# Writing the lower parts of the weights over the loaded pieces in a one-core decoder step

## The reference, cut to what matters

```python
# two groups of tokens: a prompt (512) and 8 samples of 8 tokens; 2 layers; all in float32
for layer in range(2):
    x = layer_norm(ALPHA * x + 0.5 * swiglu(x, *f1), ...)     # D_MODEL 1024, D_FF 2816
    mix = attention_and_retention(x) if layer == 0 else s5_layer(x)
    x = layer_norm(ALPHA * x + mix, ...)
    x = layer_norm(ALPHA * x + 0.5 * swiglu(x, *f2), ...)

def swiglu(x, w_gate, w_up, w_down):
    return (jax.nn.silu(x @ w_gate) * (x @ w_up)) @ w_down
```

## Time and profile before

| | |
|---|---|
| median of 3 runs | 2473.53 us (2472.99 to 2474.01) |
| profiled execution, its own time | 2471.69 us |
| its span, first to last instruction | 2470.0 us |
| granted TensorE clock, mean | 0.986 |
| PE busy | 2366.2 us (96%) |
| DVE busy | 1622.1 us (66%) |
| ACT busy | 1081.8 us (44%) |
| POOL busy | 465.0 us (19%) |
| moved by DMA | 417.85 MB, 169 GB/s on average |

### The profile page before, as it was taken

One profiled execution on the slowest core, in us unless ns is written; L12 is line 12 of the kernel. 1 busy time (PEld: TensorE's weight loads), 2 busy tenths in 40 slices (PEclk: granted clock), 3 DMA queues, 4 the chain that ended last, 5 costly groups with the idle time before them and its releaser, 6 DMA issues.

```text
span 2470.0 us, 46567 instructions
## 1 busy us (share of the span) xinstructions
PE 2366.2 (96%) x18943; PEld 2252.9 (91%) x18943; DVE 1622.1 (66%) x2539; ACT 1081.8 (44%) x1633; POOL 465.0 (19%) x535
## 2 busy tenths in 40 slices
PE   7989999999899999999999999999999999999998
PEld 6988998999789777888999999999999998999997
DVE  4796776666675656678677476477556594487555
ACT  3433344433554433452454534554333537354332
POOL 4896720000300022200202001031002010221001
PEclk9999999999999999999999999999999999999998
DMA  8667776445345798544565555555554566554553
GB/s 176 174 173 205 196 194 193 136 116 146 111 148 177 239 308 259 147 131 121 170 180 163 171 161 184 177 166 145 155 153 138 189 184 212 156 164 145 152 147 106
DMA packets 676422, 417.85 MB, mean 169 GB/s; under 512 B 31570, under 2 KB 639698, under 8 KB 676210
## 3 DMA queue, kind: packets, MB, share of 16 engines
q1 hardware_dynamic: 669682, 394.51, 55.3%
q0 software_dynamic: 6528, 20.37, 2.7%
HBM read 396.04 MB, written 18.78 MB: 168 GB/s over the span
## 4 chain that ended last, share of the span: by engine, by line
PE 76%; DVE 13%; ACT 4%; issue 3%; DMA 2%; SPq 1%; POOL 1%; DVEq 0%; ACTq 0%; POOLq 0%
PE ps L270 21%; PE ps L272 20%; PE ps L271 20%; DVE w_lo L265 4%; PE ps L1004 2%; PE ps L1006 2%; PE ps L1005 2%; ACT w_hi L256 2%; PE ps L2410 1%; DMA w_raw<-in_ffn_w_up 1%; DVE h_lo L467 1%; DVE x L557 1%; PE ps L1742 1%; PE ps L1165 1%; PE ps L2393 1%
## 5 line engine op out<-in xcount | busy, mean ns | idle before, releaser
L265 DVE TENSOR_TENSOR w_lo<-w_raw,w_hi 128x1024 fp32r<-128x1024 f32 (+1 forms) x648 | 826.8, 1280 | 612.1 <-ACT w_hi L256 608.9
L270 PE MATMUL ps<-x_hi,w_hi 128*128 128x256 f32 (+1 forms) x3200 | 970.4, 303 | 32.3 <-DVE w_lo L265 18.9
L271 PE MATMUL ps<-x_lo,w_hi 128*128 128x256 f32 (+1 forms) x3200 | 955.3, 299 | 0.0
L272 PE MATMUL ps<-x_hi,w_lo 128*128 128x256 f32 (+1 forms) x3200 | 955.1, 298 | 0.0
L256 ACT ACTIVATE w_hi<-w_raw 128x1024 fp32r<-128x1024 f32 (+1 forms) x648 | 670.3, 1035 | 582.2 <-PE ps L272 419.1
L270 PEld LDWEIGHTS ps<-x_hi,w_hi 128*128 128x128 f32 x3200 | 615.8, 192 | 50.8 <-DVE w_lo L265 35.0
L271 PEld LDWEIGHTS ps<-x_lo,w_hi 128*128 128x128 f32 x3200 | 616.0, 192 | 1.1 <-issue 0.2
L272 PEld LDWEIGHTS ps<-x_hi,w_lo 128*128 128x128 f32 x3200 | 615.6, 192 | 0.0
L270 PE MATMUL ps<-h_hi,w_hi 128*128 128x256 f32 (+1 forms) x1408 | 423.2, 301 | 14.4 <-DVE w_lo L265 10.9
L271 PE MATMUL ps<-h_lo,w_hi 128*128 128x256 f32 (+1 forms) x1408 | 414.6, 294 | 0.0
L272 PE MATMUL ps<-h_hi,w_lo 128*128 128x256 f32 (+1 forms) x1408 | 414.6, 294 | 0.0
(11 more groups left out here) (281 smaller groups left out, 2137.7 us busy)
## 6 DMA issues: line engine op xcount, KB each, us to landing
w_raw<-in_ffn_w_gate SPq DMA_DIRECT2D x176, 512.0 KB, 4.3
w_raw<-in_ffn_w_up SPq DMA_DIRECT2D x176, 512.0 KB, 3.9
w_raw<-in_ffn_w_down SPq DMA_DIRECT2D x128, 512.0 KB, 3.9
w_raw<-in_w_in_ab SPq DMA_DIRECT2D x56, 512.0 KB, 3.8
w_raw<-in_ffn_w_down SPq DMA_DIRECT2D x64, 384.0 KB, 3.3
arena<-in_cache_k SPq DMA_DIRECT2D x64, 256.0 KB, 5.1
arena<-in_cache_v POOLq DMA_DIRECT2D x64, 256.0 KB, 5.0
w_raw<-in_w_out_ab SPq DMA_DIRECT2D x16, 512.0 KB, 3.8
```

What stands on the lines that cost most here:

```text
L265: dve.tensor_tensor(T.w_lo[:, u % RING, 0:n], T.w_raw[:, u % RAW, 0:n], T.w_hi[:, u % RING, 0:n].bitcast(F32), ALU.subtract).then_inc(T.w_ ...
L270: pe.matmul(out, w_hi, m_hi, start=first, stop=False)
L271: pe.matmul(out, w_hi, m_lo, start=False, stop=False)
L272: return pe.matmul(out, w_lo, m_hi, start=False, stop=last)
```

## The change

The ring `w_raw` gets six places and lies on the same bytes as `w_lo`: the subtraction writes its result over the loaded piece. `w_hi` stays at three places, so the memory taken is the same (36 KB a partition). Of three semaphores for loads in flight nothing changes. The load of w(u) no longer waits for the subtraction of w(u-3) but for two other things: that PE is through with w(u-6), and that ACT has rounded w(u-3). `AHEAD` goes from 5 to 6.

```diff
-RAW, RING = 3, 3
+LOADING, RINGS, RING = 3, 6, 3
 LEAD = 2
...
-    T.w_raw = sb("w_raw", [P, RAW, PIECE])
     T.w_hi = sb("w_hi", [P, RING, PIECE], F32R)
-    T.w_lo = sb("w_lo", [P, RING, PIECE], F32R)
+    here = (T.nc.sbuf_base + 31) // 32 * 32
+    T.w_lo = sb("w_lo", [P, RINGS, PIECE], F32R)
+    T.w_raw = T.nc.alloc_sbuf_tensor_at("w_raw", [P, RINGS, PIECE], F32, offset=here)
...
-        dst = T.w_raw[:, u % RAW, 0:a * b].rearrange("p (a b) -> p a b", a=a)
-        if u >= RAW:
-            sp.wait_ge(T.w_split.h, u - RAW + 1)
-        sp.dma_start(dst, src).then_inc(T.w_loaded[u % RAW].h, 16)
+        dst = T.w_raw[:, u % RINGS, 0:a * b].rearrange("p (a b) -> p a b", a=a)
+        if u >= RINGS:
+            sp.wait_ge(T.w_used.h, u - RINGS + 1)
+        if u >= LOADING:
+            sp.wait_ge(T.w_rounded.h, u - LOADING + 1)
+        sp.dma_start(dst, src).then_inc(T.w_loaded[u % LOADING].h, 16)
...
-AHEAD = RAW + LEAD
+AHEAD = RINGS
...
-            load_pieces(T, sp, RAW + 8)
+            load_pieces(T, sp, LOADING + 8)
             load_tables(T, M, sp, I)
```

More of the change, by code:

```diff
@@ L187, in open_trunk @@
     T.pieces, T.banks, T.emptied, T.releases = [], [], [], {}
-    T.w_loaded = [count(f"w_loaded{i}") for i in range(RAW)]
+    T.w_loaded = [count(f"w_loaded{i}") for i in range(LOADING)]
     T.w_rounded, T.w_split, T.w_used = map(count, ("w_rounded", "w_split", "w_used"))
@@ L252, in round_piece @@
     n = T.pieces[u].shape[1] * T.pieces[u].shape[2]
-    act.wait_ge(T.w_loaded[u % RAW].h, (u // RAW + 1) * 16)
+    act.wait_ge(T.w_loaded[u % LOADING].h, (u // LOADING + 1) * 16)
     if u >= RING:
         act.wait_ge(T.w_used.h, u - RING + 1)
-    act.activation(T.w_hi[:, u % RING, 0:n], T.w_raw[:, u % RAW, 0:n], ACT.Copy).then_inc(T.w_rounded.h, 1)
+    act.activation(T.w_hi[:, u % RING, 0:n], T.w_raw[:, u % RINGS, 0:n], ACT.Copy).then_inc(T.w_rounded.h, 1)
 def rest_piece(T, dve, u):
@@ L264, in rest_piece @@
     dve.wait_ge(T.w_rounded.h, u + 1)
-    dve.tensor_tensor(T.w_lo[:, u % RING, 0:n], T.w_raw[:, u % RAW, 0:n], T.w_hi[:, u % RING, 0:n].bitcast(F32),
+    dve.tensor_tensor(T.w_lo[:, u % RINGS, 0:n], T.w_raw[:, u % RINGS, 0:n], T.w_hi[:, u % RING, 0:n].bitcast(F32),
                       ALU.subtract).then_inc(T.w_split.h, 1)
@@ L298, in columns_times @@
         cols = slice(k * P, (k + 1) * P)
-        mm = product3(pe, out, T.w_hi[:, u % RING, cols], T.w_lo[:, u % RING, cols], m_hi(k), m_lo(k),
+        mm = product3(pe, out, T.w_hi[:, u % RING, cols], T.w_lo[:, u % RINGS, cols], m_hi(k), m_lo(k),
                       first and k == 0, last and k == kt - 1)
@@ L1001, in project_tensor @@
                 x_hi, x_lo = T.x_hi[:, kk, tile_cols(t)], T.x_lo[:, kk, tile_cols(t)]
-                w_hi, w_lo = T.w_hi[:, u % RING, cols], T.w_lo[:, u % RING, cols]
+                w_hi, w_lo = T.w_hi[:, u % RING, cols], T.w_lo[:, u % RINGS, cols]
                 out = T.ps[:, bank, 0:MIX]
@@ L2945, in _ @@
                 sp.dma_start(rows[:, t], x_prompt[t * P:(t + 1) * P, :]).then_inc(T.x_loaded[t].h, 16)
-            load_pieces(T, sp, RAW)
+            load_pieces(T, sp, LOADING)
             S5C.load(sp)
```

## The result

| | before | after |
|---|---|---|
| median | 2473.46 us (2472.99 to 2474.01, 4 runs) | 2503.9 us (2498.84 to 2507.36, 4 runs) |
| ratio, 95% interval | | 1.0126 [1.0111, 1.0142] |
| profiled execution, its own time | 2471.69 us | 2507.36 us |
| its span | 2470.0 us | 2505.7 us |
| granted TensorE clock, mean | 0.986 | 0.982 |

The change makes the kernel 30.4 us (1.3%) slower. The forecast was 7 us slower, with 17 at most. The profiled execution is the slowest of its four, 3.5 us over their median, so the two traces lie 35.7 us apart, 5.3 more than the medians.

The account below looks back on a forecast made before the run. PE was taken as the bound, with hardly any idle time. Key pages +11, S5 +4 and gains -8 made +7 us on 2471.69; with 1.84 us to the median, 2480.5 us, 0.3% slower. Range -4 (2470) to +17 us (2490).

Parts of the forecast that it names:

- The cost of writing over the operand: A cost of the subtraction writing over its loaded piece, unseen and left out of the range: about one in ten.
- The tables' 2.4 us: Near 60 us: w10 and the tables go 1.3 us earlier, w11 passes two small transfers; PE's 2.4 us wait can go.
- the first term: The tables' gain of 2.4 us, which the DVE-bound stretch from 113 to 162 us may swallow.
- w53 and w54: Near 207 and 214 us: w53 goes behind eight stores instead of eight and four; PE's waits of 3.0 and 2.4 us go.
- w67: Near 258 us: its load passes twelve stores; PE's wait of 2.9 us shrinks to about 0.4, gain 2.5 us.
- all else comes from `AHEAD`: Beyond the earlier gate, each side transfer stands behind one load more: loads gain by passing it, the side work loses.
- The 1.28 us per gate: A load's gate moves from the end of a subtraction to the end of its rounding, 1.28 us earlier on average.
- The pairs with exponentials: Key pairs 10, 18 and 26, issued late behind a rounding that follows five exponentials: 1.7, 5.1 and 4.3 us lost.
- The plain pairs: Other key pairs: pair 25 issued 2.6 us late, losing 1.6 us; about half have more in hand and cost nothing.
- full price: Rival with landings as before: losses 16 + 4.7, gains 4, so +17 us, 2490; included in the forecast's 0.60.
- Taps and decays: Second S5 stretch, octets 11 to 15: decays issued later behind a load; 1.0 us at octet 11, 3.9 us in all.
- made_rows: S5 transfers near 1937 us, with 0.4 and 1.8 us in hand: 0.8 us lost.

Follow-up runs that it names:

- e1_ahead5: The changed kernel with AHEAD 5 instead of 6, shared bytes and new gates kept: 2465.01 us, ratio 0.9973 to the kernel before.
- e2_order_alone: The kernel before with AHEAD one higher (6) and nothing else: 2523.48 us, ratio 1.0208.
- e4_bytes_alone: The changed kernel with the shared bytes kept, but the old gate (subtraction of w(u-3)) and AHEAD 5: 2473.12 us, ratio 0.9999 to the kernel before.
- h2_long_holds: The kernel before with PE held nine times between 1738 and 1865 us while GpSimd writes 56 columns: 2501.0 us, ratio 1.0106.
- e3_then5: The changed kernel with AHEAD 6 early and 5 from the key pages to the end: 2463.98 us, ratio 0.9965 to the kernel before.
- h1_short_holds: The kernel before with PE held nine times between 1738 and 1865 us while GpSimd writes 14 columns: 2480.48 us, ratio 1.0021.
- e6_s5b5: The changed kernel with AHEAD 6 up to the second S5 stretch and 5 from there on: 2493.52 us, ratio 1.0083 to the kernel before.

## Why the prediction was off, point by point

**Right: the gates, the place and the sign.** The new wait for PE never decides. SP waits for ACT's rounding, where it waited for DVE:

```profile
SPq L243 <- ACT w_hi L259: 1932.4, 605, 16.1
```

605 waits in place of 607, and the same total but for 2%. `e1_ahead5` and `e2_order_alone` show that the loss sits in `AHEAD` and nowhere else, as the step said. The cost of writing over the operand, for which I had left one chance in ten, is nothing (`e4_bytes_alone`).

**Gains: 8 us forecast, 8.2 in the trace, but not by the terms: that they met is luck.** The tables' 2.4 us were won and lost again. At 114 us PE waits for DVE, which is in S5 preparation and comes late to a subtraction:

```profile
107.40 3.73 DVE L2158 COPY arena<-s_powers 128x64 f32<-128x64 f32 x8
111.29 0.91 DVE L2161 MEMSET arena<- 16x1024 f32 x1 [0.15 <-issue]
112.36 0.91 DVE L2161 MEMSET arena<- 16x1024 f32 x1 [0.16 <-issue]
113.31 3.44 DVE L268 TENSOR_TENSOR w_lo<-w_raw,w_hi 128x1024 fp32r<-128x1024 f32 x2
```

The prediction had said that the DVE-bound stretch may swallow the first term, and kept it in the 8 all the same. (`h2_long_holds`, which there is still the kernel before, has a wait of 2.8 us at this place too, so it isn't the change's alone.) The others came out larger in the shift of PE: 6.7 us instead of 5.4 for w53 and w54, 2.5 for w67. But of the 9.1 us from w48 to w72 only 4.8 are idle time, where the terms had 7.9; 4.4 are the clock, whose granted share from 200 to 265 us is 1.00 after and 0.92 before. No term had that. The waits of the earlier trace rows at 205 to 260 us were 9.0 us; those from 200 to 265 us are now

```profile
PE ps L273 <- DVE w_lo L268: 2.4, 3, 1.3
```

The cause was named wrongly in part. The step "all else comes from `AHEAD`" gave the gains to the passing of stores. But `e1_ahead5`, in which no load passes any store, has 6.7 us by its ratio. There w67 still stands behind the twelve stores, and goes at 243.92 us where it went at 250.69, since the whole queue runs ahead by the earlier gates:

```profile
237.96 5.87 SPq L2089 DMA_DIRECT2D s_made_taps<-arena  x8
243.92 0.54 SPq L244 DMA_DIRECT2D w_raw<-in_ffn_w_down  x1
```

The 1.28 us per gate, which I took for a small part, was most of it, as far as the ratios tell. The consequence is practical: the gain was to be had without the order, which cost 40 us (2503.9 against 2464.0 of `e3_then5`).

**Keys: 11 us forecast, 31.9 measured. This is the term that failed:** the sum took each page to land at most as late as before, and priced a stall of PE at its length. In three parts:

- *The pairs with exponentials* (10, 18, 26): 1.7 + 5.1 + 4.3 = 11.1 us forecast in the worked examples, 11.1 measured (pair by pair 2.5, 4.7 and 4.0). Right.
- *The plain pairs.* I had taken the landings of before for the upper bound ("if each page takes as long to land as it did"), and chose below it, since "as PE is held back the other transfers thin out". On average they did: the DMA share fell from 0.85 to 0.97 in the four windows down to 0.67 to 0.81. At pairs 15, 23 and 31 the opposite happened. There the keys meet the value pages of POOL, and being behind a load of 512 KB they are now the last of the bunch: 7.0 to 8.9 us where they took 4.3 to 5.3, 9.3 us of stalls. A landing time read from before holds only for the place in the queue that the transfer had then. Pair 25 was to cost 1.6 us and cost nothing; pairs 2 and 6 cost 3.1.
- *The clock.* No term of the sum had it. Seven stalls have PE at half clock behind them, where before there were two such places, and the same matmuls take 9.3 us longer, 9.0 of it at half clock. The rows of before had it to read: PEclk 0.96 in the windows 800 to 840 and 920 to 965 us above, with stalls of 1.9 and 1.5 us in them.

In sum 11.1 + 9.3 + 3.1 - 1.0 + 9.3 = 31.8 us, in this trace. The 16 us of the "full price" had neither the second nor the last of these.

**S5: 4 us forecast, 10.3 measured.** Taps and decays were 3.9 us; PE's waits for decays are now 4.5 us in 4 places, about right. `made_rows`, forecast at 0.8, cost 3.4:

```profile
PE ps L2413 <- DMA arena<-s_made_decays: 4.5, 4, 1.7
...
PE ps L2359 <- issue: 3.4, 4, 1.2
```

(before had no wait for a transfer at either line there). The eight `made_rows` take 4.5 to 7.0 us to land, before 4.4 to 6.5, and all eight are issued later against PE; the longest waits, 0.9 and 1.2 us, are at the two slowest landings, the fourth (6.5) and the eighth (7.0), which took 4.6 before. Another 2.0 us is PE's longer busy time, 174.5 us for what took 172.5; 1.5 of it falls into stretches at half clock. The last 1.6 us of the balance is the clock alone. Near 1052 us before and 1076 after, PE has the same stall of 2.7 us for DVE; the windows around it, before and then after:

```profile
1044.00:1064.00 20.00, 17.31 (x83) 14.24 (x82) 15.74 (x27) 11.71 (x22) 0.00 (x0) 1.00 0.35 101
```

```profile
1068.00:1088.00 20.00, 17.30 (x76) 14.06 (x75) 14.88 (x27) 11.83 (x22) 0.00 (x0) 0.91 0.26 76
```

**The rivals.** None held. "The full price" was the nearest, 14 us short. It failed for the same two reasons as the forecast: bounds taken from durations of before don't bound a queue whose order is changed, and stalls were priced at their length.

**What stays open:** why the clock drops behind one stall of 1.5 to 3 us and not behind another, and in one execution and not in another behind the same stall. And what the order brings in the early stretch beyond the gates (`e3_then5` against `e1_ahead5`) is smaller than these runs can tell.

## What to carry to other kernels

When a queue's order is changed, treat each landing time as a property of the place in the queue. Look at what else is in flight at that moment, on every queue, and who is now the last of the bunch. Price a stall of TensorE of 1.5 us and more at its length plus, if the clock drops, 1.5 to 2.7 us more, and read from several traces how often it does: one trace can have been lucky, as that of before was at 848 us. And where one edit does two things (here an earlier gate and a later place), ask for each what it earns alone; here the gate alone earned 6.7 us, and with the order changed only where it does no harm 8.7, which these runs can't tell apart.

## What the runs showed of the hardware

- A stall too short to lower the clock costs 0.3 us more than its wait: 0.90 us for 0.6, nine times over.
- A short drop of the clock costs 1.5 to 1.6 us: 3.9 against 2.4 us at holds of 2.0 to 2.2 us, and +1.6 us at the stall of 2.7 us that both traces have. Four of nine holds of nearly equal length had one. A drop of twice the length cost 2.7 us (`h1_short_holds` against before, from w216 to w220), behind a stall of 3.2 us that had it in five of eight traces, a short one in one and none in two.
- An elementwise operation that writes over its own operand takes the time of one that doesn't (1281 against 1280 ns).
- With a quarter of the bytes in each value page, the pages of keys land in a median of 4.3 us instead of 4.8; but at the three places where all transfers meet the difference is 2.8 to 4.6 us (1.8 to 3.1 against `e6_s5b5`). A median of landings hides just the ones that count.
